# Start of the gated delta rule put in another order: key roots and decay rows beside the last input products, keys normalised before the masks, pooled rows split at other places

## The chip, the cores and the metric

One core of one Trainium2 chip runs the whole program. The metric is the device time of one execution in microseconds (us). PE is TensorE, ACT is ScalarE, DVE is VectorE, POOL is GpSimd, SP is SyncE. PSUM is the accumulator memory of eight banks, each 128 partitions by 512 fp32 values.

## The reference, cut to what matters

Two transformer blocks run over 256 tokens of width 2048. The first begins with a mixer: one product `p = h @ w_in` (5136 columns) gives the pooled part `u`, the gate logits and q, k, v, z of a gated delta net with 8 heads of 128. The delta net, in chunks of 64 tokens:

```python
qkv = silu(causal_dwconv(concat([q, k, v]), conv_w))
q = l2_normalize(q) * Dh ** -0.5
k = l2_normalize(k)
beta = sigmoid(b_logit)
g = -exp(a_log) * softplus(a_logit + dt_bias)
gc = cumsum(g within a chunk)
decay = exp(where(causal, gc[i] - gc[j], -inf))
l_mat = where(strict, beta[i] * (k k^T) * decay, 0)
sol = triangular_solve(l_mat, [v * beta, k * beta * exp(gc)])   # unit diagonal
attn = (q k^T) * decay
q_dec = q * exp(gc); k_dec = k * exp(gc[-1] - gc); chunk_decay = exp(gc[-1])
# then a scan over the 4 chunks, a norm, a gate by silu(z)
```

The mixer's output is `concat([y_pool, y_dn]) @ w_mix_out`. Cross attention, a feed-forward part and a second block with its own attention and feed-forward part follow; nothing in them is touched by the change.

## The kernel before, in words

**Large products.** A fp32 product is made of three fp32r products. `product` (lines 866 to 868) multiplies the split activation (`hhi`, `hlo`) by a weight split into `whi` and `wlo`. SP loads weights in units of four 128-row tiles into four `raw` slots; ACT casts half a unit to `whi` (`split_hi`, line 1322), DVE subtracts to get `wlo` (`split_lo`, line 1813), and PE multiplies. The four `whi` and four `wlo` buffers are the eight 1024-column pieces of `ring`. Results go to the four banks of `GP`: even blocks to banks 0 and 1, odd blocks to banks 2 and 3, and ACT copies them to `p1` (`store`, line 1399), which counts `evac0` for even and `evac1` for odd blocks.

**Input product.** The phases wi0 to wi4 are w_in, wi4 the last. Beside them run the pooling, the gate inputs and six groups of the convolution. For group g: PE turns q/k/v columns into bank pair `TA` (`conv_turn`), ACT makes the first tap (`tap`), DVE adds three taps (`conv`, semaphore `cv_c`), ACT takes the sigmoid into `csg` (`conv_sigmoid`, line 1448, `cv_s`), POOL multiplies (line 756, `cv_m`), PE turns back into `TB` (`conv_back`, `cv_b`), ACT stores into `p1` (`conv_store`, line 1453, `cv_e`). The order is written by hand: `todo` tables on PE, ACT and DVE say behind which unit of which phase each step stands. The number is a unit count; 28 to 31 are units of wi4, and 32 stands behind the cast of its last unit. Two steps of group 5 (sigmoid and store on ACT, `conv_back(5)` on PE) stand behind wi4.

**Delta rule, beginning.** Tokens are two halves (`hf`) of 128, each holding two chunks; all eight heads of a half are handled at once in tiles of 128 by 8 by 128. `AB[hf]` are the two PSUM bank pairs of a half: `TA` and `TB` for half 0, `GP` 0-1 and `GP` 2-3 for half 1. `DN[hf]` names the SBUF tiles (KB, KBT, KT, QT, DT, LT, YY, TT, MT, AA). For half 0 the first eight lie in `ring`, and MT is `flat`. For half 1 they lie in the arena where the pooling and convolution buffers were. The steps in the order before:

1. PE: sums of the log decays, 16 products of 8 columns (`dn_sum`, line 997); then `conv_back(5)`; then differences of log decays, two products of 512 and eight of 128 columns in each half of a bank pair (`dn_diff`, lines 1006 and 1010), which read a row tile that DVE writes (`dn_tg`, line 1967, into KB).
2. ACT: `conv_sigmoid(5)`, `conv_store(5)`, square roots of the key and query norms (`dn_rt`, line 1483), two casts of pooled rows to `hhi` (`pool_hi`, line 1486), exponentials of the sums (`dn_ex`, line 1489), exponentials of the masked differences (`dn_dt`, line 1492).
3. DVE: masks (`dn_dm`, line 1970), then per half: reciprocal, keys normalised (line 1975), keys times beta into KB (`dn_kb`, line 1976), queries normalised (`dn_qn`, line 1978).
4. PE: turns of k and KB (`dn_t`), ACT copies (`dn_tc`, line 1503) to KT and KBT; turns of q, copies to QT; products KT by KBT (`dn_lt_mm`, line 1031) and KT by QT (`dn_at_mm`, line 1036); turns of the decayed q (copies in halves, lines 1500 and 1501).
5. DVE: L (`dn_lt`, line 1982), q times its decay (`dn_qd`, line 1986), the remainder of the pooled rows into `hlo` (`pool_lo`, line 1992), the attention weights (`dn_at`, line 1995).
6. POOL masks L by level (line 761, `lv_m`). PE turns the first level (`lv_z`), DVE subtracts it from the identity (lines 2000 and 2001), and five levels of two products each invert the triangle (lines 1059 and 1072; DVE line 2009).

The solution, the scan over chunks (lines 1084 to 1115) and the product with `w_mix_out` follow. Its first units are the pooled rows and wait for `pool_lo`.

Of the kernel before, what the change touches and what calls it, by code (L numbers as in the profile page):

```python
# [6 lines left out]
F32 = mybir.dt.float32  # L7
F32R = mybir.dt.float32r
ALU = mybir.AluOpType
ACT = mybir.ActivationFunctionType  # L10
# [136 lines left out]
def program(nc, A, out):  # L147
    PH = plan()
    order = list(PH.values())
    with ExitStack() as ctx:  # L150
# [119 lines left out]
        def hd(hf, j):  # L270
# [6 lines left out]
              dict(zip(keys, late[0:7] + [hd(1, 0), late[7], late[2], late[2]]))]  # L277
        ar = Arena(); ar.at = norm_at
# [560 lines left out]
        def _(pe):  # L839
# [122 lines left out]
            def conv_back(g):  # L962
                pe.wait_ge(S("cv_m"), g + 1)
                if g:
                    pe.wait_ge(S("cv_e"), g)
                else:
                    pe.wait_ge(S("pool_f"), 4)
                for h in range(NH):
                    for f in range(4):
                        m = turn(TB[:, h * 512 + f * P:h * 512 + f * P + P], cbuf[g % 3][:, f, h * P:h * P + P])  # L970
                m.then_inc(S("cv_b"), 1)
# [72 lines left out]
            for hf in range(NH):  # L1044
                pe.wait_ge(S("dn_at"), hf + 1)
# [28 lines left out]

            level(0, False, False)
# [235 lines left out]
        def _(act):  # L1311
# [138 lines left out]
            def conv_store(g):  # L1450
                act.wait_ge(S("cv_b"), g + 1)
                c = QKV + 512 * g
                nc.scalar.copy(p1[:, :, c:c + 512], v(TB, 512)).then_inc(S("cv_e"), 1)
# [8 lines left out]
                    30: [lambda it: conv_store(4)]}  # L1462
# [9 lines left out]
            conv_sigmoid(5)  # L1472
# [8 lines left out]
            for hf in range(NH):  # L1481
                act.wait_ge(S("dn_ms"), hf + 1)
                nc.scalar.activation(r16[hf], m16[hf], ACT.Sqrt).then_inc(S("dn_rt"), 1)
            hp = hhi[:, 0:8, :].rearrange("p (a f) t -> p f a t", f=2)
            for f in range(2):
                nc.scalar.copy(hp[:, f, :, :], p1[:, f, 0:1024].rearrange("p (a t) -> p a t", t=T)).then_inc(S("pool_hi"), 1)
            for hf in range(NH):
                act.wait_ge(S("dn_sum"), hf + 1)
                nc.scalar.activation(ex[hf], AB[hf][0][:, 0, 0:32], ACT.Exp).then_inc(S("dn_ex"), 1)
# [3 lines left out]
            for step in ((0, 1), (2,), (3,)):  # L1493
                for hf in range(NH):
                    for j in step:
                        act.wait_ge(S("dn_t"), 2 * hf + j + 1 if j < 2 else hf + 2 * j + 1)
# [16 lines left out]

            level(0, False)
# [269 lines left out]
        def _(dve):  # L1784
# [152 lines left out]
            def squares(hf, i):  # L1937
# [4 lines left out]

            todo = {12: [lambda it: gate_first()], 14: [lambda it: gate_second()], 19: [lambda it: squares(0, 0)],
                    23: [lambda it: squares(1, 0)], 27: [lambda it: squares(0, 1)], 31: [lambda it: squares(1, 1)]}
# [9 lines left out]
            dve.wait_ge(S("gp_b"), 1)  # L1954

# [6 lines left out]
            for hf in range(NH):  # L1962
                nc.vector.tensor_scalar(m16[hf], s16[hf], EPS, None, ALU.add).then_inc(S("dn_ms"), 1)
            for e in range(2):
                dve.wait_ge(S(f"evac{e}"), 1 + PH["wi4"].ev1)
            for hf in range(NH):
                TTo(DN[hf]["KB"], rows(C("upto"), 8), cols(gdec[:, hf * 8:hf * 8 + 8], P), ALU.mult).then_inc(S("dn_tg"), 1)
# [3 lines left out]
            for hf in range(NH):  # L1971
                q3, k3 = hd(hf, 0), hd(hf, 1)
                dve.wait_ge(S("dn_rt"), hf + 1)
                link(nc.vector.reciprocal(i16[hf], r16[hf]))
                link(TTo(k3, k3, cols(i16[hf][:, 8:16], P), ALU.mult))
                TTo(DN[hf]["KB"], k3, cols(beta[:, hf * 8:hf * 8 + 8], P), ALU.mult).then_inc(S("dn_kb"), 1)
                link(nc.vector.tensor_scalar(i16[hf][:, 0:8], i16[hf][:, 0:8], P ** -0.5, None, ALU.mult))
# [9 lines left out]
            for hf in range(NH):  # L1987
                if hf == 0:
                    hp, lp = (t[:, 0:8, :].rearrange("p (a f) t -> p f a t", f=2) for t in (hhi, hlo))
                    for f in range(2):  # L1990
                        dve.wait_ge(S("pool_hi"), f + 1)
                        TTo(lp[:, f, :, :], p1[:, f, 0:1024].rearrange("p (a t) -> p a t", t=T), hp[:, f, :, :].bitcast(F32),
                            ALU.subtract).then_inc(S("pool_lo"), 1)
# [19 lines left out]
            level(4, "AA")  # L2013

# [365 lines left out]
```

## Time and profile before

| | us |
|---|---|
| median of three runs | 2829.23 |
| lowest and highest | 2820.55, 2829.27 |
| the profiled execution's own time | 2826.76 |
| span of its trace | 2825.0 |
| last product of wi4 begins | 259.14 |
| first level of the inversion begins on DVE | 303.70 |
| first product with w_mix_out begins | 381.29 |

All times in rows are us from the start of the span unless they are marked ns. A timeline row has start, duration, engine, line, operation, output<-inputs, shapes and count, and in brackets how long the engine had been idle before it and who ended that. The share of a granted clock of 1.00 is the upper level of TensorE's clock.

### The profile page before, as it was taken

The numbers are of one execution on the slowest core, as the hardware profiler recorded it, in microseconds if no ns is written. First come the engines' busy times: TensorE is split into PE (matmuls) and PEld (weight loads), VectorE is DVE, ScalarE is ACT, GpSimd is POOL, SyncE is SP. The second block draws the span as 40 slices with busy tenths as digits, with TensorE's granted clock in tenths as the row PEclk, the third lists the DMA queues.
The fourth block names the chain that finished last, engine by engine and source line by source line (L and its number), as shares of the span: only waits on it lengthen the run. The fifth ranks groups of instructions, "written<-read, shape, count | busy, mean of one in ns | idle before, by whom it ended". The sixth has DMA issues, their size and how long they took to land.

```text
span 2825.0 us, 34772 instructions
## 1 busy us (share of the span) xinstructions
PE 2742.2 (97%) x13302; PEld 2342.0 (83%) x13302; DVE 1776.7 (63%) x2014; ACT 1326.9 (47%) x1678; POOL 169.6 (6%) x132
## 2 busy tenths in 40 slices
PE   8998899999899999999999999998989999999998
PEld 8998888888788888888888889887778888888886
DVE  4466578676558887865555564546775756644555
ACT  5554354454335545434554544436454444344453
POOL 0001620000000000000000000820000000000000
PEclk9999999999999999999999999999999999999999
DMA  8553048887557787776555556650655866755553
GB/s 282 161 174 122 1 182 286 292 269 267 193 173 269 273 283 265 285 253 194 193 189 197 186 184 201 200 169 5 226 192 182 282 220 226 266 189 180 188 188 119
DMA packets 293266, 579.60 MB, mean 205 GB/s; under 512 B 9168, under 2 KB 46192, under 8 KB 292112
## 3 DMA queue, kind: packets, MB, share of 16 engines
q1 hardware_dynamic: 291296, 566.08, 59.9%
q0 software_dynamic: 1120, 8.57, 0.7%
q10 hardware_dynamic: 720, 3.15, 0.3%
q8 instruction: 90, 1.47, 0.2%
q14 instruction: 40, 0.33, 0.0%
HBM read 575.66 MB, written 2.10 MB: 205 GB/s over the span
## 4 chain that ended last, share of the span: by engine, by line
PE 95%; DVE 3%; ACT 1%; issue 1%; DMA 0%; POOL 0%; SPq 0%; DVEq 0%; ACTq 0%
PE GP L866 28%; PE GP L868 28%; PE GP L867 28%; PE TA L841 2%; PE TB L841 2%; PE TB L489 1%; PE GP L466 1%; PE TA L1229 0%; PE GP L841 0%; DVE x L2248 0%; PE TA L1072 0%; PE GP L1072 0%; PE GP L1059 0%; DMA x<-in_x 0%; PE TA L1279 0%
## 5 line engine op out<-in xcount | busy, mean ns | idle before, releaser
L1813 DVE TENSOR_TENSOR wlo<-raw,whi 128x1024 fp32r<-128x1024 f32 (+2 forms) x904 | 1088.2, 1217 | 811.1 <-ACT whi L1322 801.9
L1322 ACT CAST whi<-raw 128x1024 fp32r<-128x1024 f32 (+2 forms) x904 | 925.8, 1031 | 1167.9 <-PE GP L868 1113.9
L866 PE MATMUL GP<-whi,hhi 128*128 128x512 f32 (+2 forms) x1792 | 688.8, 384 | 3.4 <-issue 2.9
L868 PE MATMUL GP<-whi,hlo 128*128 128x512 f32 (+2 forms) x1792 | 680.3, 380 | 0.0
L867 PE MATMUL GP<-wlo,hhi 128*128 128x512 f32 (+2 forms) x1792 | 679.9, 379 | 0.0
L866 PEld LDWEIGHTS GP<-whi,hhi 128*128 128x128 f32 x1792 | 337.8, 188 | 54.2 <-issue 4.9
L868 PEld LDWEIGHTS GP<-whi,hlo 128*128 128x128 f32 x1792 | 337.3, 188 | 52.0
L867 PEld LDWEIGHTS GP<-wlo,hhi 128*128 128x128 f32 x1792 | 337.8, 189 | 50.3 <-issue 1.0
L866 PE MATMUL GP<-whi,bhi 128*128 128x512 f32 x704 | 276.7, 393 | 0.2 <-DVE blo L1874 0.2
L1801 DVE SCALAR_TENSOR_TENSOR ada_acc<-raw,csig,ada_acc 128x512 f32<-128x512 f32 x360 | 270.3, 751 | 10.2
L868 PE MATMUL GP<-whi,blo 128*128 128x512 f32 x704 | 274.3, 390 | 0.0
L867 PE MATMUL GP<-wlo,bhi 128*128 128x512 f32 x704 | 273.9, 389 | 0.0
L866 PE MATMUL GP<-whi,f2hi 128*128 128x512 f32 x512 | 201.4, 393 | 0.0
L868 PE MATMUL GP<-whi,f2lo 128*128 128x512 f32 x512 | 199.4, 389 | 0.0
L867 PE MATMUL GP<-wlo,f2hi 128*128 128x512 f32 x512 | 199.2, 389 | 0.0
L868 PEld LDWEIGHTS GP<-whi,blo 128*128 128x128 f32 x704 | 132.1, 188 | 27.8
L866 PEld LDWEIGHTS GP<-whi,bhi 128*128 128x128 f32 x704 | 132.2, 188 | 27.2 <-DVE blo L1874 0.7
L867 PEld LDWEIGHTS GP<-wlo,bhi 128*128 128x128 f32 x704 | 132.3, 188 | 26.5
L866 PE MATMUL GP<-whi,fhi 128*128 128x512 f32 x352 | 137.3, 390 | 0.0
L868 PE MATMUL GP<-whi,flo 128*128 128x512 f32 x352 | 137.0, 389 | 0.0
L867 PE MATMUL GP<-wlo,fhi 128*128 128x512 f32 x352 | 136.9, 389 | 0.0
L866 PEld LDWEIGHTS GP<-whi,f2hi 128*128 128x128 f32 x512 | 96.1, 188 | 20.6 <-issue 1.0
(420 smaller groups left out, 2590.8 us busy)
## 6 DMA issues: line engine op xcount, KB each, us to landing
raw<-in_w_up SPq DMA_DIRECT2D x108, 1024.0 KB, 5.4
raw<-in_w_down SPq DMA_DIRECT2D x108, 1024.0 KB, 5.1
raw<-in_w_ada SPq DMA_DIRECT2D x96, 1024.0 KB, 5.3
raw<-in_w_gate SPq DMA_DIRECT2D x44, 1024.0 KB, 5.3
raw<-in_w_in SPq DMA_DIRECT2D x48, 856.0 KB, 4.8
raw<-in_w_xkv SPq DMA_DIRECT2D x32, 1024.0 KB, 5.7
raw<-in_w_in SPq DMA_DIRECT2D x24, 1024.0 KB, 5.1
raw<-in_w_in SPq DMA_DIRECT2D x24, 864.0 KB, 4.7
```

Of the source, the lines that this page charges most:

```text
L466: m = pe.matmul(o[:, h * T:h * T + u["L"]], l, r, start=(d == 0), stop=(d == n - 1), skip_group_check=True)
L489: m = pe.matmul(bank[:, j * P:j * P + P], l, r, start=(d == 0), stop=(d == len(terms) - 1), skip_group_check=True)
L841: return pe.transpose(dst, src, ident[0:n, 0:n] if n != P else ident)
L866: pe.matmul(o, ahi[:, kt, t], whi[r][:, k, 0:q.width], start=first, stop=False)
L867: pe.matmul(o, ahi[:, kt, t], wlo[r][:, k, 0:q.width], start=False, stop=False)
L868: m = pe.matmul(o, alo[:, kt, t], whi[r][:, k, 0:q.width], start=False, stop=last)
L1322: nc.scalar.copy(whi[(2 * g + s) % NRING][:, :, 0:q.width], raw[j % NSLOT][:, 2 * s:2 * s + 2, 0:q.width])\
L1801: m = nc.vector.scalar_tensor_tensor(ada_acc[:, :], raw[j % NSLOT][:, k, :], c, ada_acc[:, :], ALU.mult, ALU.add)
L1813: TTo(wlo[r][:, :, 0:q.width], raw[j % NSLOT][:, 2 * s:2 * s + 2, 0:q.width], whi[r][:, :, 0:q.width].bitcast(F32), ALU.subtract).then_inc ...
```

## The change

On PE, `conv_back(5)` goes ahead of the sums and writes `TA` instead of `TB`. The sums of both halves go to `GP` bank 0 and wait for `evac0` alone. The differences read `TG`, a new name for two tiles (MT of half 0, KBT of half 1). The turns of k of both halves come ahead of those of KB, the turns of q of both ahead of the first products. The wait for `dn_at` is ahead of the first level, no longer ahead of the turns of MT.

On ACT, `conv_sigmoid(5)` stands behind unit 31, the square roots (`key_roots`) at 32, ahead of the last `store`. The two casts of pooled rows stand just ahead of the levels. The copies go by step and half rather than by half and step for the first two.

On DVE, `square_means` follows the last squares, the decay rows are written before the delta rule's other steps, without a wait for `evac`. Keys are normalised and multiplied by beta ahead of the masks, queries behind them. The pooled remainders stand behind the last level.

```diff
+        TG = [DN[0]["MT"], DN[1]["KBT"]]
@@ PE
+                back = TB if g < 5 else TA
+                if g == 5:
+                    pe.wait_ge(S("cv_c"), 6)
...
-            for e in range(2):
-                pe.wait_ge(S(f"evac{e}"), 1 + PH["wi4"].ev1)
-            pe.wait_ge(S("cv_c"), 6)
+            conv_back(5)
+            pe.wait_ge(S("evac0"), 1 + PH["wi4"].ev1)
             for hf in range(NH):
                 for j, m_ in enumerate(("upto", "after", "chunk0", "chunk1")):
-                    m = pe.matmul(AB[hf][0][:, 0, 8 * j:8 * j + 8], C(m_), gdec[:, hf * 8:hf * 8 + 8], start=True, stop=True)
+                    m = pe.matmul(GP[:, 0, 32 * hf + 8 * j:32 * hf + 8 * j + 8], C(m_), gdec[:, hf * 8:hf * 8 + 8], start=True, stop=True)
                 m.then_inc(S("dn_sum"), 1)
-            conv_back(5)
             for hf in range(NH):
-                KB, B8 = DN[hf]["KB"], AB[hf][1]
+                KB, B8 = TG[hf], AB[hf][1]
                 if hf == 0:
-                    pe.wait_ge(S("cv_e"), 6)
+                    pe.wait_ge(S("cv_e"), 5)
+                else:
+                    pe.wait_ge(S("evac1"), 1 + PH["wi4"].ev1)
...
             for hf in range(NH):
-                pe.wait_ge(S("dn_ex"), hf + 1)
+                pe.wait_ge(*((S("dn_ex"), 2) if hf else (S("cv_e"), 6)))
                 pe.wait_ge(S("dn_kb"), hf + 1)
                 for h in range(8):
                     m = turn(AB[hf][0][:, h, :], hd(hf, 1)[:, h, :])
                 m.then_inc(S("dn_t"), 1)
+            for hf in range(NH):
                 pe.wait_ge(S("dn_dm"), hf + 1)
...
-                pe.wait_ge(S("dn_tc"), 2 * hf + 1)
+                pe.wait_ge(S("dn_tc"), hf + 1)
                 pe.wait_ge(S("dn_qn"), hf + 1)
...
-                pe.wait_ge(S("dn_tc"), 2 * hf + 2)
+            for hf in range(NH):
+                pe.wait_ge(S("dn_tc"), hf + 3)
...
             for hf in range(NH):
-                pe.wait_ge(S("dn_at"), hf + 1)
                 pe.wait_ge(S("dn_tc"), hf + 7)
...
+            pe.wait_ge(S("dn_at"), 2)
             level(0, False, False)
@@ ACT
+            def key_roots():
+                for hf in range(NH):
+                    act.wait_ge(S("dn_ms"), hf + 1)
+                    nc.scalar.activation(r16[hf], m16[hf], ACT.Sqrt).then_inc(S("dn_rt"), 1)
...
-                    30: [lambda it: conv_store(4)]}
+                    30: [lambda it: conv_store(4)], 31: [lambda it: conv_sigmoid(5)], 32: [lambda it: key_roots()]}
...
-            conv_sigmoid(5)
             conv_store(5)
...
             for hf in range(NH):
-                act.wait_ge(S("dn_sum"), hf + 1)
-                nc.scalar.activation(ex[hf], AB[hf][0][:, 0, 0:32], ACT.Exp).then_inc(S("dn_ex"), 1)
+                act.wait_ge(S("dn_sum"), 2)
+                nc.scalar.activation(ex[hf], GP[:, 0, 32 * hf:32 * hf + 32], ACT.Exp).then_inc(S("dn_ex"), 1)
...
-            for step in ((0, 1), (2,), (3,)):
+            for step in ((0,), (1,), (2,), (3,)):
...
+            hp = hhi[:, 0:8, :].rearrange("p (a f) t -> p f a t", f=2)
+            for f in range(2):
+                nc.scalar.copy(hp[:, f, :, :], ...).then_inc(S("pool_hi"), 1)      # removed ahead of dn_ex
             level(0, False)
@@ DVE
-                    ..., 31: [lambda it: squares(1, 1)]}
+                    ..., 31: [lambda it: (squares(1, 1), square_means())]}
...
             dve.wait_ge(S("gp_b"), 1)
+            decay_rows()              # TG[hf] = upto * gdec, dn_tg
...
             for hf in range(NH):
+                k3 = hd(hf, 1)
+                dve.wait_ge(S("dn_rt"), hf + 1)
+                link(nc.vector.reciprocal(i16[hf], r16[hf]))
+                link(TTo(k3, k3, cols(i16[hf][:, 8:16], P), ALU.mult))
+                if hf == 0:
+                    for e in range(2):
+                        dve.wait_ge(S(f"evac{e}"), 1 + PH["wi4"].ev1)
+                TTo(DN[hf]["KB"], k3, cols(beta[:, hf * 8:hf * 8 + 8], P), ALU.mult).then_inc(S("dn_kb"), 1)
+                link(nc.vector.tensor_scalar(i16[hf][:, 0:8], i16[hf][:, 0:8], P ** -0.5, None, ALU.mult))
             for hf in range(NH):
                 dve.wait_ge(S("dn_diff"), hf + 1)
                 TTo(DN[hf]["DT"], AB[hf][1], rows(C("chunk_mask"), 8), ALU.add).then_inc(S("dn_dm"), 1)
             for hf in range(NH):
-                ...                   # the key steps above stood here
+                q3 = hd(hf, 0)
                 TTo(q3, q3, cols(i16[hf][:, 0:8], P), ALU.mult).then_inc(S("dn_qn"), 1)
...
             level(4, "AA")
+            for f in range(2):        # removed ahead of dn_at
+                dve.wait_ge(S("pool_hi"), f + 1)
+                TTo(lp[:, f, :, :], ..., hp[:, f, :, :].bitcast(F32), ALU.subtract).then_inc(S("pool_lo"), 1)
+            dve.wait_ge(S("pool_lo"), 2)
```

## Rows read from the trace of the kernel before

**Rows 1.** The page's chain that ended last, share of the span by engine.

```profile
PE 95%; DVE 3%; ACT 1%; issue 1%; DMA 0%; POOL 0%; SPq 0%; DVEq 0%; ACTq 0%
```

**Rows 2.** Windows: length, busy us of PE, PEld, DVE, ACT, POOL, PEclk, DMA share, GB/s.

```profile
260.00:264.00 4.00, 1.92 (x16) 1.86 (x16) 3.23 (x2) 1.61 (x3) 2.31 (x1) 1.00 0.00 0
264.00:268.00 4.00, 2.65 (x9) 1.82 (x10) 1.27 (x1) 1.98 (x2) 0.19 (x1) 0.57 0.01 4
276.00:280.00 4.00, 0.43 (x4) 0.24 (x3) 3.46 (x4) 1.06 (x1) 0.00 (x0) 1.00 0.00 0
280.00:284.00 4.00, 2.61 (x16) 2.24 (x16) 3.90 (x6) 1.85 (x2) 0.00 (x0) 0.70 0.00 0
310.00:352.00 42.00, 41.08 (x366) 40.89 (x367) 13.54 (x20) 18.43 (x35) 32.25 (x24) 1.00 0.00 1
400.00:440.00 40.00, 40.00 (x188) 33.24 (x187) 33.83 (x41) 20.50 (x25) 0.44 (x1) 1.00 0.97 352
```

**Rows 3.** Timeline of PE, from the last product of wi4 to the differences.

```profile
259.14 0.36 PE L868 MATMUL GP<-whi,hlo 128*128 128x428 f32 x1
260.92 1.03 PE L997 MATMUL TA<-small,cst 128*128 128x8 f32 x8 [1.42 <-ACT p L1399]
264.25 1.72 PE L841 MATMUL TB<-cst,cbuf 128*128 128x128 f32 x8 [1.40 <-POOL cbuf L756]
267.06 2.08 PE L1006 MATMUL TB<-ring,cst 128*128 128x512 f32 x2 [1.10 <-ACT p L1453]
...
272.76 1.02 PE L1006 MATMUL GP<-t,cst 128*128 128x512 f32 x2
...
275.38 1.05 PE L1010 MATMUL GP<-cst,t 128*128 128x128 f32 x8
```

**Rows 4.** Timeline of PE, from the key products to the first level.

```profile
289.09 1.95 PE L1031 MATMUL TB<-ring 128*128 128x128 f32 x16
...
297.11 1.04 PE L841 MATMUL TB<-cst,p 128*128 128x128 f32 x8
...
302.55 1.97 PE L841 MATMUL TB<-cst,flat 128*128 128x128 f32 x8 [3.53 <-DVE ring L1995]
...
306.39 1.16 PE L1059 MATMUL TA<-ring,flat 128*128 128x128 f32 x8 [0.45 <-POOL flat L761]
```

**Rows 5.** Timeline of ACT, 250 to 299 us.

```profile
250.25 0.91 ACT L1322 CAST whi<-raw 128x856 fp32r<-128x856 f32 x1 [1.36 <-PE GP L868]
259.54 1.13 ACT L1399 ACTIVATE p<-GP,small 128x428 f32<-128x428 f32 x2 [8.37 <-PE GP L868]
260.55 1.06 ACT L1448 ACTIVATE csg<-cbuf 128x1024 f32<-128x1024 f32 x1
...
267.03 1.28 ACT L1483 ACT_TABLE_LOAD   x1
...
277.73 1.06 ACT L1492 ACTIVATE t<-t 128x1024 f32<-128x1024 f32 x1 [2.45 <-DVE t L1970]
281.62 1.01 ACT L1503 COPY ring<-TA 128x1024 f32<-128x1024 f32 x1 [2.83 <-PE TA L841]
...
298.18 0.59 ACT L1500 COPY ring<-TB 128x512 f32<-128x512 f32 x1 [5.22 <-PE TB L841]
```

**Rows 6.** Timeline of POOL, 261 to 296 us.

```profile
261.69 2.50 POOL L756 TENSOR_TENSOR cbuf<-cbuf,csg 128x1024 f32<-128x1024 f32 x1 [21.99 <-ACT csg L1448]
292.45 3.41 POOL L761 TENSOR_TENSOR flat<-ring,cst 128x512 f32<-128x512 f32 x2 [28.26 <-DVE ring L1982]
```

**Rows 7.** Timeline of DVE, 252 to 361 us.

```profile
252.16 1.22 DVE L1940 TENSOR_TENSOR flat<-p 128x1024 f32<-128x1024 f32 x1
...
261.91 3.36 DVE L1967 TENSOR_TENSOR t<-cst,small 128x1024 f32<-128x1024 f32 x1
...
276.47 1.23 DVE L1970 TENSOR_TENSOR t<-GP,cst 128x1024 f32<-128x1024 f32 x1 [2.28 <-PE GP L1010]
...
291.15 1.23 DVE L1982 TENSOR_TENSOR ring<-TB,ring 128x1024 f32<-128x1024 f32 x1 [5.41 <-PE TB L1031]
...
296.87 4.49 DVE L1992 TENSOR_TENSOR hlo<-p,hhi 128x1024 fp32r<-128x1024 f32 x2
...
303.70 0.69 DVE L2000 TENSOR_TENSOR ring<-cst,TB 128x512 f32<-128x512 f32 x1
...
360.66 0.69 DVE L2034 COPY p<-TB 128x512 f32<-128x512 f32 x1 [7.54 <-PE TB L1112]
```

More of the change, by code:

```diff
@@ L967, in conv_back @@
                     pe.wait_ge(S("pool_f"), 4)
+                back = TB if g < 5 else TA
+                if g == 5:
+                    pe.wait_ge(S("cv_c"), 6)
                 for h in range(NH):
                     for f in range(4):
-                        m = turn(TB[:, h * 512 + f * P:h * 512 + f * P + P], cbuf[g % 3][:, f, h * P:h * P + P])
+                        m = turn(back[:, h * 512 + f * P:h * 512 + f * P + P], cbuf[g % 3][:, f, h * P:h * P + P])
                 m.then_inc(S("cv_b"), 1)
@@ L1452, in conv_store @@
                 c = QKV + 512 * g
-                nc.scalar.copy(p1[:, :, c:c + 512], v(TB, 512)).then_inc(S("cv_e"), 1)
+                nc.scalar.copy(p1[:, :, c:c + 512], v(TB if g < 5 else TA, 512)).then_inc(S("cv_e"), 1)
+            def key_roots():
+                for hf in range(NH):
+                    act.wait_ge(S("dn_ms"), hf + 1)
+                    nc.scalar.activation(r16[hf], m16[hf], ACT.Sqrt).then_inc(S("dn_rt"), 1)
             todo = {2: [lambda it: pool_mean(0)], 3: [lambda it: tap(0)], 4: [lambda it: (pool_out(0), pool_mean(1))],
@@ L1481, in _ @@
             for hf in range(NH):
[L1482 to L1487, printed above, removed]
-                act.wait_ge(S("dn_sum"), hf + 1)
-                nc.scalar.activation(ex[hf], AB[hf][0][:, 0, 0:32], ACT.Exp).then_inc(S("dn_ex"), 1)
+                act.wait_ge(S("dn_sum"), 2)
+                nc.scalar.activation(ex[hf], GP[:, 0, 32 * hf:32 * hf + 32], ACT.Exp).then_inc(S("dn_ex"), 1)
             for hf in range(NH):
@@ L1492, in _ @@
                 nc.scalar.activation(DN[hf]["DT"], DN[hf]["DT"], ACT.Exp).then_inc(S("dn_dt"), 1)
-            for step in ((0, 1), (2,), (3,)):
+            for step in ((0,), (1,), (2,), (3,)):
                 for hf in range(NH):
                     for j in step:
-                        act.wait_ge(S("dn_t"), 2 * hf + j + 1 if j < 2 else hf + 2 * j + 1)
+                        act.wait_ge(S("dn_t"), hf + 2 * j + 1)
                         if j == 3:
@@ L1512, in level @@
                             nc.scalar.copy(DN[hf]["AA"][:, a, :], AB[hf][1][:, a, :]).then_inc(S("lv_ac"), 1)
+            hp = hhi[:, 0:8, :].rearrange("p (a f) t -> p f a t", f=2)
+            for f in range(2):
+                nc.scalar.copy(hp[:, f, :, :], p1[:, f, 0:1024].rearrange("p (a t) -> p a t", t=T)).then_inc(S("pool_hi"), 1)
             level(0, False)
@@ L1941, in squares, with square_means, decay_rows @@
                 link(nc.vector.tensor_reduce(s16[hf][:, 8 * i:8 * i + 8], sq, AX.X, ALU.add))
+            def square_means():
+                for hf in range(NH):
+                    nc.vector.tensor_scalar(m16[hf], s16[hf], EPS, None, ALU.add).then_inc(S("dn_ms"), 1)
+            def decay_rows():
+                for hf in range(NH):
+                    TTo(TG[hf], rows(C("upto"), 8), cols(gdec[:, hf * 8:hf * 8 + 8], P), ALU.mult).then_inc(S("dn_tg"), 1)
             todo = {12: [lambda it: gate_first()], 14: [lambda it: gate_second()], 19: [lambda it: squares(0, 0)],
-                    23: [lambda it: squares(1, 0)], 27: [lambda it: squares(0, 1)], 31: [lambda it: squares(1, 1)]}
+                    23: [lambda it: squares(1, 0)], 27: [lambda it: squares(0, 1)], 31: [lambda it: (squares(1, 1), square_means())]}
             for g, at in enumerate((4, 8, 16, 20, 24, 28)):
@@ L1962, in _ @@
             for hf in range(NH):
[L1963 to L1967, printed above, removed]
+                k3 = hd(hf, 1)
[7 more added lines that the diff above has]
+                link(nc.vector.tensor_scalar(i16[hf][:, 0:8], i16[hf][:, 0:8], P ** -0.5, None, ALU.mult))
             for hf in range(NH):
@@ L1971, in _ @@
             for hf in range(NH):
[L1972 to L1977, printed above, removed]
+                q3 = hd(hf, 0)
                 TTo(q3, q3, cols(i16[hf][:, 0:8], P), ALU.mult).then_inc(S("dn_qn"), 1)
@@ L1987, in _ @@
             for hf in range(NH):
[L1988 to L1993, printed above, removed]
                 dve.wait_ge(S("dn_at_mm"), hf + 1)
@@ L2013, in _ @@
             level(4, "AA")
+            hp, lp = (t[:, 0:8, :].rearrange("p (a f) t -> p f a t", f=2) for t in (hhi, hlo))
+            for f in range(2):
+                dve.wait_ge(S("pool_hi"), f + 1)
+                TTo(lp[:, f, :, :], p1[:, f, 0:1024].rearrange("p (a t) -> p a t", t=T), hp[:, f, :, :].bitcast(F32),
+                    ALU.subtract).then_inc(S("pool_lo"), 1)
+            dve.wait_ge(S("pool_lo"), 2)
             def new_values(n):
```

## The prediction, made before the changed kernel was run

> **What bounds the kernel now.** I read the chain that ended last first: 95% of it is TensorE, so time is to be had only where TensorE stands still or runs slowly [rows 1]. The windows then show where that is. In the 40 us after the product with w_mix_out has begun, PE is busy 40.00 of 40.00, and in the levels of the inversion 41.08 of 42.00, both at the upper clock of 2.4 GHz; between them and the end of w_in it is not: 1.92 of 4.00 in 260 to 264, 0.43 of 4.00 in 276 to 280. Behind each of these two idle windows the granted clock is down, 0.57 and 0.70 as means of a stretch that is partly at 1.2 GHz [rows 2]. Third, the timelines of the engines between 259 and 304 say who holds PE: ACT's store, POOL's product of group 5, ACT's store of that group [rows 3], then DVE, which makes masks and keys one behind the other, and at the end again DVE, where the turn of MT waits 3.53 us for the attention weights [rows 4] behind the pooled remainders (two in 4.49 us) [rows 7]. From 303.70, where DVE begins the first level, DVE, POOL and PE run a fixed pattern that the change leaves alone. So the sum is one date: when does DVE begin that level?
>
> The remaining wi4 products end at 259.50 in either kernel (last row 259.14, 0.36 long, the next instruction can begin at about 259.35) [rows 3].
>
> **Part 1, up to the differences.** Removed from the path: 1.42 us for the store, 1.40 us for POOL, 1.10 us for ACT's store of group 5 [rows 3]. For that the sigmoid must be early. The last cast ends at 251.16 and ACT is then idle for 8.37 us until 259.54 [rows 5]: the sigmoid runs 251.1 to 252.2 (1.06), POOL multiplies until 254.7 (2.50) [rows 6]. Cover is 4.6 us against the turn at 259.35; without it the turn would wait as before. The roots stand ahead of the last store in ACT's queue, so a late root would hold `evac1`. DVE's squares begin at 252.16 (product 1.22, reduction about as long), the means are there at 255.0, table load (1.28) already past, roots done at 255.3. Should POOL's product hold DVE's first square, it costs at most the 2.14 us that the decay row lost in the same company (3.36 instead of 1.22) [rows 7]: roots at 257.5, still 2 us early. Nothing is queued behind but the store itself. The decay rows (2 times 1.14 behind each other) are there at 257.4, at worst 259.6; PE asks at 262. The first key product is then done at 259.9 at the latest or waits one pitch more; KB of half 0 starts when the store ends, 260.77, KB of half 1 is there at 265 (or 266).
>
> PE's new path: eight turns from 259.35, 0.87 us at the upper clock as the turns of q show by start to start (1.04 long, with 0.17 overlap) [rows 4]: 260.2. Sixteen sums: eight took 0.88 start to start, so 1.76 [rows 3]: 262.0. Their bank 0 was emptied long before. Differences: half 1 took 272.76 to 276.43, 3.67 us, at the upper clock; half 0 took 267.06 to 272.76, 5.70 us, partly at the lower [rows 3]. I take 3.6 for each, since PE now has no gap from 259 on: 269.2, against 276.43 before. This step is 7.2 us earlier, of it 3.9 from idle time, 0.9 from the turns (1.72 to 0.87), 2.1 from the differences, and the rest handovers. Bounds: if both differences run as the first did before, 273.4; the least is 3.5 each, 269.0.
>
> The clock is the one unmeasured thing here. In the rows the lower level follows windows in which PE was busy for a half or less [rows 2]. The Trainium skill, TensorE: Matmul & The Clock Gate, Part 1, says that the clock is held at its lower level by default and released by activity, according to how busy TensorE was; the trace agrees so far. By that rule the removal of the gaps brings the 2.4 GHz that I take. The same section calls the moment of the switch variable from run to run. If that moment, and not the gaps, rules here, the cost stays, and that is the first rival.
>
> **Part 2, masks and keys.** Before, mask 1, reciprocal, key product, KB and query of half 0 and then of half 1 lay between the differences and the key products: 276.43 to 289.09, 12.7 us. Now only the mask, an exponential and ACT's copies do. From the end e = 269.2: DVE masks half 1 at e + 0.0, ACT's exponential begins e + 1.3 (276.47 to 277.73 in the rows [rows 5, 7]) and frees ACT at e + 2.3; KT0, KT1 and KBT0 are copied, 0.95 apart and the last 1.01 long [rows 5]: e + 5.2. PE meanwhile turns k (2 times 0.87), KB (2 times 0.87), q of half 0 behind KT0's copy, q of half 1 behind KT1's at e + 4.2 to e + 5.1. ACT and PE arrive together, so the product KT by KBT of half 0 begins at e + 5.3 = 274.5, 14.6 us earlier than 289.09 [rows 4]. ACT's store of group 5, the exponential's table (1.28) and `dn_ex` are done at 263.4, under the differences (PE asks at 270.1); without that cover 1.3 us more. DVE's two query products (1.14 each) end at e + 3.5, before their turns. What is late next is ACT: a bound above is PE waiting for all four copies, 0.95 more; below, PE's turns alone, e + 4.5.
>
> **Part 3, up to the first level.** Products of L, half 0 and half 1, and of attention, half 0 and half 1: each 16 matmuls in 1.79 us start to start (1.95 long) [rows 4]. 274.5 + 4 times 1.79 + 0.15 = 281.8. Decayed q turned: ACT begins its two half copies 1.07 us after the turn began (297.11, 298.18) and needs 0.48 + 0.59 [rows 4, 5]: 284.0. PE turns the first half of MT, 0.45, and with the handover DVE can begin at 284.65. DVE's own line: L0 at 276.6 (2.06 behind PE's start, 289.09 to 291.15 [rows 4, 7]), decayed q0 277.7, L1 278.85, decayed q1 280.0 to 281.2, or until 282.4 if POOL's two maskings (3.41 with DVE in the way, 1.2 each alone [rows 6]) hold it; attention weights of half 0 and half 1 behind PE at 281.9, or until 284.7. Both lines end at about 284.7. Before it was 303.70 [rows 7]: **19.0 us earlier**. Left out of this line are the pooled remainders: 4.49 us on DVE [rows 7]. They go behind the last level, where DVE is idle 7.54 us before the scan [rows 7]; they need about 2.3 us there, because POOL is idle too. If that cover were gone, up to 4.5 us return. The casts go to ACT between 285 and 287; its first copy of a level comes 1.2 us behind PE's first product, which moves from 306.39 to 287.4 [rows 4]: cover about 1.6 us, and if it is missed, 1 us at most. The removed wait for `dn_at` costs nothing where it now stands: DVE has passed it by then.
>
> **Sum.** Everything behind depends on what runs before it and on no fixed date, transfers included: the four slots of w_mix_out were filled by 258, and the later ones are issued as slots come free. The profiled execution took 2826.76 us; 2826.76 - 19.0 = 2807.8. The median of the three runs is 2829.23, 2.5 above that execution, and gives 2810.2. I predict 2809. The steps' bounds add up to a gain of 14.8 (differences at the lower clock) to 20 us (PE's turns alone).
>
> **Rivals.**
> First, *the clock still falls*. The sums have eight columns and PE does little in them. If they count as idleness, the differences run at 1.2 GHz: half 0 needs 5.7 instead of 3.6, half 1 the same: 4.2 us lost, 2813. For: the fall before came behind exactly these sums. Against: behind 1.42, 1.40 and 1.10 us of idleness too, which go.
> Second, *the gain doesn't arrive*. A transfer or another engine has its own date: the stretch behind carries 352 GB/s at a DMA share of 0.97 [rows 2]. If it were bound by transfers, starting 19 us earlier would show as waits of PE: 2829, or 2821 to 2835 as the three runs scatter. Against: PE busy 40.00 of 40.00 there, and no transfer of it beyond the four slots can start before the delta rule is over, so the ratio of the two doesn't change.
> Third, *slower*. The levels run close to saturation at 1.00 [rows 2]. If the new order started them at 1.2 GHz and the pattern's short gaps kept the clock there, each us of the levels' PE work costs one more. It decides from 19 us of such work on; over all of the 41.08 us the balance is +22, 2849 for 2827. For: the first products of the levels come singly with gaps of 0.7 us. Against: the same gaps stood there before, behind the same turns, and the clock was 1.00.
>
> **How the numbers follow.** Forecast as summed 0.78; clock still falls 0.11 (also faster); gain doesn't arrive 0.07; slower 0.04. A measurement of this kernel can tell about 0.3%, 8.5 us, from no change. Faster by more: 0.90 (0.78 + 0.11, and what of the second lands beyond the bound); within: 0.06; slower: 0.04. The range goes from 2800 (the lowest run, 2820.55, less 20) to 2818 (the highest, 2829.3, less 15, and some of what the second rival might take).
>
> **What would show it.** One row each in the profile of the changed kernel: turns from `cbuf` right behind the last wi4 product and lasting 0.9; granted clock 1.00 from 256 to 276; L1006's successor beginning at 262; the key products at 274 to 275; the first level on DVE at 284 to 286; PE's first w_mix_out product at 362 instead of 381.29; DVE's remainders in the gap before the scan. It is wrong if the sigmoid of group 5 or the roots end behind 259, if the clock is at 0.5 in the differences, or if the first w_mix_out product is early and the end is not.

## The result and the profile after

| | before | after |
|---|---|---|
| median of five runs, us | 2828.34 | 2801.84 |
| lowest and highest | 2817.66, 2829.27 | 2800.70, 2810.06 |
| profiled execution's own time | 2826.76 | 2801.02 |
| span of its trace | 2825.0 | 2799.2 |
| from the last wi4 product to the first level on DVE | 44.56 | 25.30 |
| from the last wi4 product to the first w_mix_out product | 122.15 | 102.88 |
| from there to the end of the span | 2443.7 | 2436.7 |

The two medians are 26.5 us apart. The ratio on record, 0.9931, with a 95% interval from 0.9906 to 0.9956, is 19.5 us, between 12 and 27; the reason why the two differ stands below, with the last seven microseconds. The interval leaves out 1, so the changed kernel is faster, by less than 1%. The chain is still 95% PE. PE's timeline now runs without a hole from wi4 to the turn of MT.

```profile
260.06 1.13 ACT L1405 ACTIVATE p<-GP,small 128x428 f32<-128x428 f32 x2 [3.50 <-PE GP L869]
...
283.15 0.59 ACT L1504 COPY ring<-TB 128x512 f32<-128x512 f32 x1 [5.63 <-PE TB L842]
```

These are two rows of ACT's timeline of the changed kernel; PE's, with the last wi4 product first, is:

```profile
259.67 0.36 PE L869 MATMUL GP<-whi,hlo 128*128 128x428 f32 x1
259.86 1.03 PE L842 MATMUL TA<-cst,cbuf 128*128 128x128 f32 x8
260.73 1.85 PE L1000 MATMUL GP<-small,cst 128*128 128x8 f32 x16
262.44 1.10 PE L1010 MATMUL TB<-flat,cst 128*128 128x512 f32 x2
...
266.02 1.02 PE L1010 MATMUL GP<-t,cst 128*128 128x512 f32 x2
...
269.53 1.04 PE L842 MATMUL TA<-cst,p 128*128 128x128 f32 x8
...
274.85 2.03 PE L1037 MATMUL TB<-ring 128*128 128x128 f32 x16
...
284.28 1.09 PE L842 MATMUL TB<-cst,flat 128*128 128x128 f32 x8 [0.29 <-ACT ring L1505]
...
287.71 1.13 PE L1064 MATMUL TA<-ring,flat 128*128 128x128 f32 x8 [1.36 <-issue]
```

Against [rows 3, 4] the three idle stretches of 1.42, 1.40 and 1.10 us ahead of the differences are gone, and L1037, which stood at 289.09 as L1031, stands at 274.85. The turn from `cbuf` begins 0.19 us behind the start of the last product and lasts 1.03 us (0.87 to the next start), where it lasted 1.72 us before [rows 3].

The windows of the changed kernel (length, busy of PE, PEld, DVE, ACT, POOL, PEclk, DMA share, GB/s):

```profile
256.00:260.00 4.00, 4.00 (x23) 3.84 (x22) 3.93 (x7) 0.32 (x2) 0.17 (x1) 1.00 0.36 137
260.00:264.00 4.00, 4.00 (x33) 3.52 (x32) 2.78 (x5) 3.60 (x6) 0.00 (x0) 1.00 0.00 0
264.00:268.00 4.00, 4.00 (x25) 3.01 (x25) 2.71 (x4) 0.45 (x1) 0.00 (x0) 1.00 0.00 0
284.00:288.00 4.00, 2.36 (x18) 2.04 (x19) 3.03 (x4) 3.09 (x5) 2.49 (x2) 1.00 0.00 0
293.00:333.00 40.00, 39.66 (x356) 39.66 (x357) 12.59 (x19) 18.01 (x34) 31.10 (x23) 1.00 0.00 1
362.00:366.00 4.00, 3.53 (x10) 2.76 (x9) 4.00 (x3) 1.00 (x1) 2.58 (x1) 0.57 0.25 43
380.00:420.00 40.00, 40.00 (x186) 33.18 (x186) 34.02 (x41) 20.52 (x25) 0.77 (x1) 1.00 0.94 346
```

Where [rows 2] had 1.92 busy of 4.00 and then a clock of 0.57, there is now 4.00 of 4.00 and 1.00. The product with w_mix_out is as busy as before (40.00 of 40.00), so the 19 us are not given back there. The window from 362 to 366, with its start, ran at 0.57 in this execution; the first four us of that product ran at 1.00 in the profile of the kernel before (381.29 to 385.29) and in the second one of the changed kernel (362.29 to 366.29).

DVE's timeline of the changed kernel shows what became of its work:

```profile
256.39 1.22 DVE L1956 TENSOR_TENSOR flat<-cst,small 128x1024 f32<-128x1024 f32 x1
...
261.32 1.23 DVE L1986 TENSOR_TENSOR ring<-p,small 128x1024 f32<-128x1024 f32 x1 [1.15 <-ACT p L1405]
...
269.73 1.23 DVE L1990 TENSOR_TENSOR t<-GP,cst 128x1024 f32<-128x1024 f32 x1 [2.21 <-PE GP L1014]
...
280.39 1.22 DVE L2001 TENSOR_TENSOR p<-p,small 128x1024 f32<-128x1024 f32 x1
...
284.97 0.69 DVE L2009 TENSOR_TENSOR ring<-cst,TB 128x512 f32<-128x512 f32 x1 [1.10 <-PE TB L842]
...
334.29 2.35 DVE L2026 TENSOR_TENSOR hlo<-p,hhi 128x1024 fp32r<-128x1024 f32 x2
341.99 1.52 DVE L2049 COPY p<-TB 128x512 f32<-128x512 f32 x2 [5.34 <-PE TB L1118]
```

The first level (L2009) waits 1.10 us for PE instead of following the attention weights; before, DVE was the last to come [rows 7]. The two remainders take 2.35 us where they took 4.49 [rows 7], and DVE still idles 5.34 us behind them.

### The profile page after: what moved, and what is told of

Same layout as the page of the kernel before. It is cut to its first block, busy times and chain, and to the rows that moved or that the text cites. A ratio compares the mean times of both kernels' runs of the same rounds, so it can differ in the third digit from the quotient of the medians.

```text
span 2799.2 us, 34774 instructions
## 1 busy us (share of the span) xinstructions
PE 2727.0 (97%) x13302; PEld 2328.3 (83%) x13302; DVE 1772.5 (63%) x2014; ACT 1324.0 (47%) x1678; POOL 169.6 (6%) x132
## 4 chain that ended last, share of the span: by engine, by line
PE 95%; DVE 3%; ACT 1%; issue 1%; DMA 0%; SPq 0%; POOL 0%; DVEq 0%; ACTq 0%
PE GP L867 29%; PE GP L869 28%; PE GP L868 28%; PE TA L842 2%; PE TB L842 2%; PE TB L490 1%; PE GP L467 1%; PE TA L1235 0%; DVE x L2263 0%; DVE wlo L1820 0%; PE GP L1077 0%; PE TA L1077 0%; PE GP L1064 0%; PE GP L842 0%; DMA x<-in_x 0%
## 5 line engine op out<-in xcount | busy, mean ns | idle before, releaser
L868 PEld LDWEIGHTS GP<-wlo,f2hi 128*128 128x128 f32 x512 | 96.1, 188 | 20.6 <-issue 1.0
```

Source lines behind the costliest of these rows:

```text
L868: pe.matmul(o, ahi[:, kt, t], wlo[r][:, k, 0:q.width], start=False, stop=False)
```

## The experiments

Each experiment below was profiled once. Most are read by one distance, from the start of the last wi4 product to the first level on DVE (44.56 us before, 25.30 after, 25.30 again in a second profile of the changed kernel; 44.56 and 43.99 for the two profiles of the kernel before). It contains nothing but the part that was changed, and it repeats to 0.6 us or better, where a single whole time can be 10 us off. Read up to the first w_mix_out product instead, each distance gives nearly the same comparison, at most 1.1 us away: gap_one, for one, has 6.03 us there instead of 4.99, chiefly because 16 matmuls of its scan took 3.63 us where the changed kernel took 2.05.

| kernel | distance | beside its neighbour | first w_mix_out product to the end |
|---|---|---|---|
| before, twice | 44.56, 43.99 | | 2443.7, 2444.8 |
| after, twice | 25.30, 25.30 | | 2436.7, 2445.0 |
| gaps_back | 31.66 | after + 6.36 | 2445.9 |
| gap_one | 30.29 | after + 4.99 | 2445.9 |
| sigmoid_late | 35.54 | after + 10.24 | 2435.2 |
| roots_late | 26.14 | after + 0.84 | 2436.1 |
| keys_late | 33.74 | after + 8.44 | 2444.6 |
| pooled_old | 28.56 | after + 3.26 | 2435.9 |
| sigmoid_alone | 41.49 | before - 3.07 | 2445.9 |
| keys_alone | 35.73 | before - 8.83 | 2445.9 |
| pooled_alone | 40.80 | before - 3.76 | 2436.1 |
| identity_ahead | see below | | 2443.6 |

### Does the clock fall because of the gaps?

**gaps_back** puts waits of PE back into the changed kernel:

```diff
+            for e in range(2):
+                pe.wait_ge(S(f"evac{e}"), 1 + PH["wi4"].ev1)
             conv_back(5)
-            pe.wait_ge(S("evac0"), 1 + PH["wi4"].ev1)
+            pe.wait_ge(S("cv_e"), 6)
```

> The changed kernel, but PE waits for the last store of wi4 before it turns group 5 back, and for the store of group 5 before the sums: two short gaps as before, about 1.4 and 1.0 us, nothing else moved. Distance from the last wi4 product to the first level on DVE: 25.30 us in the changed kernel. Theory (idle gaps make the clock fall): granted clock at 1.2 GHz somewhere in the differences, distance 25.3 + 2.4 + 2 to 4 = 30 to 32 us. Rival (the moment rules, not the gaps): clock stays at 2.4 GHz, distance 27.7. Stretch from the first w_mix_out product to the end of the span: 2436.7 us in the changed kernel, 2443.7 in the one before; if the difference of 7.0 comes from the change it is 2436 to 2437 here, if it is scatter of the clock it is anything from 2432 to 2447.

31.66 us: the two gaps, 1.48 and 1.10 us of idleness, put off what stands behind them by 1.65 and 1.30 us, and the lower clock makes up the remaining 3.4 of the 6.36. **gap_one** keeps only the first:

```diff
+            for e in range(2):
+                pe.wait_ge(S(f"evac{e}"), 1 + PH["wi4"].ev1)
             conv_back(5)
-            pe.wait_ge(S("evac0"), 1 + PH["wi4"].ev1)
```

> The changed kernel, but PE waits for the last store of wi4 before it turns group 5 back: one gap of about 1.4 us, the second gap of gaps_back (1.10 us) is not there. Question: how little idleness brings the fall. If one such gap is enough, the granted clock falls in the differences as in gaps_back (31.66 us) and the distance is 29 to 31 us; if it takes both, the clock stays at 2.4 GHz and the distance is 26.7.

One gap is enough. PE's timeline and the windows of gap_one:

```profile
261.47 1.06 PE L842 MATMUL TA<-cst,cbuf 128*128 128x128 f32 x8 [1.48 <-issue]
262.37 2.73 PE L1001 MATMUL GP<-small,cst 128*128 128x8 f32 x16
264.95 2.06 PE L1011 MATMUL TB<-flat,cst 128*128 128x512 f32 x2
```

```profile
256.00:260.00 4.00, 3.99 (x21) 3.53 (x19) 3.93 (x7) 0.32 (x2) 0.13 (x1) 1.00 0.34 132
260.00:264.00 4.00, 2.53 (x20) 2.56 (x20) 2.78 (x5) 2.54 (x4) 0.00 (x0) 0.89 0.02 4
264.00:268.00 4.00, 4.00 (x14) 2.97 (x14) 1.44 (x3) 1.17 (x3) 0.00 (x0) 0.50 0.00 0
268.00:272.00 4.00, 4.00 (x18) 2.61 (x17) 0.75 (x1) 0.00 (x0) 0.00 (x0) 0.76 0.00 0
```

The sums take 2.73 instead of 1.85 us and the first two products of the differences 2.06 instead of 1.10; of the 4.99 us 1.65 are the gap (the turn begins 1.84 us behind the last product instead of 0.19) and 3.3 the lower clock. Beside gap_one, the second gap of gaps_back costs 1.37 us, which is about its own length. The rival by which the moment alone rules falls: in the six profiles with PE unbroken here (after twice, roots_late, pooled_old, keys_late, identity_ahead) the granted clock was 1.00 from 256 to 268, and in the eight with a gap there it fell each time, before 268. No run has this short gap without the narrow sums behind it, so what share these have is not shown. And a gap alone doesn't decide either. Behind the turn of MT the changed kernel has gaps of 1.36, 0.72, 0.74 and 0.73 us. In its first profile the clock stayed at 1.00 there; in the second it fell at 289 and cost nothing, since PE waits for POOL there anyway (distance from the last wi4 product to the second product of level 0: 34.67 and 34.70).

### The sigmoid and the roots beside the last products

**sigmoid_late** takes both steps out of the tables:

```diff
-    30: [lambda it: conv_store(4)], 31: [lambda it: conv_sigmoid(5)], 32: [lambda it: key_roots()]}
+    30: [lambda it: conv_store(4)]}
...
+            conv_sigmoid(5)
             conv_store(5)
+            key_roots()
```

> The changed kernel, but the sigmoid of group 5 and the square roots of the norms stand behind the last store of wi4 again. Theory: PE's turn of group 5 waits until about 5 us behind the last wi4 product (store 1.0, sigmoid 1.06, POOL 2.5), keys wait for the roots (about 9 us behind it), the clock falls: distance to the first level 31.5 to 34 us instead of 25.3. Rival (the beginning is covered by the later chain of ACT copies and DVE): under 28 us. Stretch behind the first w_mix_out product: as said for the first run, 2436 to 2437 or scattered.

35.54 us, above the range of the theory. PE stands 4.74 us, until POOL's product is there (262.90, 2.34 long), and then does the turn, the sums and the first half of the differences at the lower clock; from the turn to the end of the differences 15.0 us pass instead of 9.7. The later start, 4.9 us, and the slower course, 5.3, are the whole 10.24:

```profile
265.45 1.94 PE L842 MATMUL TA<-cst,cbuf 128*128 128x128 f32 x8 [4.74 <-issue]
267.18 3.42 PE L1000 MATMUL GP<-small,cst 128*128 128x8 f32 x16
```

**roots_late** puts only `key_roots()` back behind `conv_store(5)` (the hook 32 goes, the sigmoid's stays).

> The changed kernel, but the square roots stand behind the store of group 5; the sigmoid stays early. It parts the 10.2 us that sigmoid_late cost (35.54 against 25.30). Theory: roots at 264 instead of 256, KB of half 1 at 269 instead of 265.4, masks behind it; PE has work until 269.5, so distance 26 to 27.5 us, and most of the 10.2 belongs to the sigmoid. Rival (the roots were the greater part): 30 us or more.

26.14 us, 0.84 more. The early roots are worth under 1 us, because PE has work of its own until 269.5. What the late roots put off is DVE's first mask (269.78 instead of 266.30), with it ACT's exponentials and copies, and PE waits once, for the first copy:

```profile
274.18 1.09 PE L842 MATMUL TA<-cst,p 128*128 128x128 f32 x8 [0.64 <-ACT ring L1508]
```

With the roots late, the late sigmoid costs another 9.4 us (35.54 against 26.14).

**sigmoid_alone** is the same move in the kernel before: `31: [lambda it: conv_sigmoid(5)]` added, the call behind wi4 removed.

> The kernel before with one part of the change: the sigmoid of group 5 stands behind unit 31 instead of behind the last store. PE's order is the old one, so the turn of group 5 now follows the sums at once, about 3.6 us behind the last wi4 product instead of 5.1. Theory (the parts help mostly together): differences begin 2.4 us earlier, distance to the first level 40 to 42.5 us instead of 44.56. Rival (POOL's product was the wait of the whole beginning): under 39 us.

41.49 us, 3.07 less. The same step that costs 9.4 us when it is undone in the changed kernel is worth 3.07 in the kernel before. There the gaps of 1.42 and 1.10 us remain, and the lower clock with them: the granted clock of sigmoid_alone was 0.62 and 0.52 in 264 to 268 and 268 to 272.

### Keys ahead of the masks

**keys_late** exchanges two blocks on DVE in the changed kernel: the masks (`dn_dm`) first, then the key steps.

> The changed kernel, but DVE normalises the keys and makes KB behind the masks. Theory: PE waits for KB of half 0 about 4 us, LT begins 5 us later, and the idle stretch brings 1.2 GHz for a part: distance 30.5 to 33 us instead of 25.3. Rival (ACT's exponentials and copies bound that stretch anyway): under 27.5 us.

33.74 us. The theory holds; the distance lies 0.7 us above its range. PE stands 4.09 us for the first KB, and then, which I had not priced, 1.70 us for the second; the rest, about 2.5 us, is the lower clock on the turns behind, as two of its windows show.

```profile
272.00:276.00 4.00, 1.19 (x8) 0.85 (x8) 3.90 (x5) 1.04 (x2) 0.00 (x0) 0.92 0.00 0
276.00:280.00 4.00, 2.56 (x12) 2.59 (x13) 3.71 (x5) 1.37 (x2) 0.00 (x0) 0.50 0.00 0
```

```profile
277.44 1.94 PE L842 MATMUL GP<-cst,p 128*128 128x128 f32 x8 [1.70 <-DVE t L1989]
```

**keys_alone** does it in the kernel before:

```diff
+        TG = [DN[0]["MT"], DN[1]["KBT"]]
-                KB, B8 = DN[hf]["KB"], AB[hf][1]
+                KB, B8 = TG[hf], AB[hf][1]
-                TTo(DN[hf]["KB"], rows(C("upto"), 8), ...).then_inc(S("dn_tg"), 1)
+                TTo(TG[hf], rows(C("upto"), 8), ...).then_inc(S("dn_tg"), 1)
+            (reciprocal, key product, KB and scaling of both halves)
             (masks of both halves)
+            (queries of both halves)
```

> The kernel before with one part of the change: DVE normalises the keys and makes KB ahead of the masks (decay rows in the tiles of TG, at their old time; roots, pooled rows, sigmoid and PE's order as before). Theory: half of the work between the differences and LT goes under the differences; DVE waits for the roots until 268.6, masks end at about 276.5, LT begins about 5 us earlier: distance 38 to 41 us instead of 44.56. Rival (without early roots the keys only trade places with the masks): 43 us or more.

35.73 us, better than expected: 8.83 us of the 19.26. I had let the masks hold PE, but when the differences end both KB are there (DVE is done with the second at 276.21), and PE turns keys at once (277.65, right behind the last difference of 276.76). In the kernel before, PE stood twice at that place:

```profile
280.52 1.06 PE L841 MATMUL TA<-cst,p 128*128 128x128 f32 x8 [4.09 <-DVE ring L1976]
284.54 1.94 PE L841 MATMUL GP<-cst,p 128*128 128x128 f32 x8 [1.41 <-DVE t L1976]
```

So 5.5 of the 8.83 us are idle time, and most of the other 3.3 are the lower clock of the turns (0.50 in 284 to 288 before; 1.00 from 276 to 292 in keys_alone). This part needs neither early roots nor a new order of PE.

### The pooled rows

**pooled_old** puts casts and remainders back to their old places in the changed kernel, **pooled_alone** moves them in the kernel before; both edits are the pooled lines of the change, one backwards.

> The changed kernel, but the casts of the pooled rows stand ahead of the exponentials of the sums on ACT, and the pooled remainders ahead of the attention weights on DVE, as before. Theory: DVE begins the attention weights 2.3 to 4.5 us later (POOL masks beside it), the first level begins 3.3 us later: distance 28 to 29.5 us. Rival (the remainders fit into DVE's gaps and the level is set by PE and ACT): under 26.5 us.

> The kernel before with one part of the change: casts of the pooled rows ahead of the levels on ACT, remainders behind the last level on DVE. Undoing it in the changed kernel cost 3.26 us (28.56 against 25.30). Theory (the part is additive): distance 40 to 41.5 us instead of 44.56. Rival (it is worth more beside the others): 43 us or more.

28.56 us (3.26 more than after) and 40.80 (3.76 less than before): additive within 0.5 us, as expected. In pooled_old DVE needs 4.51 us for the pair:

```profile
282.18 4.51 DVE L2005 TENSOR_TENSOR hlo<-p,hhi 128x1024 fp32r<-128x1024 f32 x2
286.61 1.21 DVE L2009 TENSOR_TENSOR ring<-TA,ring 128x1024 f32<-128x1024 f32 x1
```

and 2.35 in the place where POOL rests (it stands idle for 18.66 us up to 342.76). POOL's two masks beside the 4.51 us took 4.47 us; in the changed kernel they took 2.52, beside DVE products of which one input comes from PSUM (L2004, 1.21 and 1.22). The Trainium skill, SBUF — State Buffer, section "Who interferes with whom", says that a DVE instruction with two inputs in SBUF contends with a GpSimd instruction that reads SBUF, and calls their shared port pair an exclusive lock; the durations agree with that.

### Where the other seven microseconds come from

> The changed kernel once more, as it is. Distance from the last wi4 product to the first level on DVE 25.3 us, as in its first profile (fixed by the program). Stretch from the first w_mix_out product to the end: 2436.7 in its first profile. Theory (the 7.0 us beyond the predicted 19 are scatter of TensorE's clock in later stages): anything from 2432 to 2447, with the time at the lower clock to match, and a ratio of 0.991 to 0.996. Rival (they come from the change): 2436 to 2437 again, ratio 0.990 to 0.991.

> The kernel before once more, as it is. Distance 44.6 us. Stretch behind the first w_mix_out product 2443.7 in its first profile. Scatter theory: anything from 2432 to 2447. Rival: 2443 to 2444 again.

The changed kernel again: 2801.53 us median of six (2801.15 to 2810.89), ratio 0.9928, interval 0.9904 to 0.9951, so by its expectation the ratio is inside the scatter theory's band. Its profile gives 2445.0 us behind the first w_mix_out product, not 2436.7: one program, two values 8.3 us apart, so the rival of after_again falls. The kernel before again gives 2444.8, near its first 2443.7, and tells nothing by itself. Over all 14 profiles the stretch is 2435.2 to 2436.7 in five and 2443.6 to 2445.9 in nine, and it does not go with the date at which it begins: pooled_alone begins it at 379.32 with 2436.1, the second profile of the changed kernel at 362.29 with 2445.0. Windows of the changed kernel's first and second profile, over the two attention stages and the one behind:

```profile
725.00:800.00 75.00, 64.95 (x358) 56.83 (x357) 34.03 (x42) 26.93 (x44) 0.00 (x0) 0.95 0.35 121
1895.00:1995.00 100.00, 86.59 (x513) 73.02 (x514) 71.86 (x139) 56.27 (x165) 0.00 (x0) 0.98 0.24 80
2050.00:2100.00 50.00, 37.78 (x178) 31.63 (x177) 37.07 (x60) 29.42 (x48) 0.00 (x0) 0.90 0.40 136
```

```profile
725.00:800.00 75.00, 64.96 (x337) 56.52 (x337) 31.79 (x39) 24.31 (x42) 0.00 (x0) 0.89 0.30 101
1895.00:1995.00 100.00, 87.88 (x498) 76.64 (x497) 66.77 (x138) 52.96 (x158) 0.00 (x0) 0.90 0.18 64
2050.00:2100.00 50.00, 38.35 (x178) 32.19 (x178) 40.20 (x66) 28.23 (x49) 0.00 (x0) 0.86 0.45 149
```

Over the same microseconds of nearly the same work the mean clock is 0.95 or 0.89, 0.98 or 0.90, 0.90 or 0.86. The whole executions have 0.993 and 0.988; as an estimate, 0.005 of 2800 us is 14 us of work at the upper clock, which is room enough for the 8.3, since a part of the lower clock falls on waits. The mean granted clock of a whole run sorts the times of one kernel too. In the later series of 11 runs the kernel before ran five times with 0.983 (2829.3 to 2830.2 us, mean 2829.9) and five times with 0.989 or 0.990 (2816.1 to 2820.6, mean 2818.1), and once with 0.986 (2827.6); the changed kernel, in its 11 of both series, seven times with 0.991 to 0.993 (2800.7 to 2801.8, mean 2801.3) and four times with 0.988 to 0.990 (2807.8 to 2810.9, mean 2809.5). Upper group against upper group the change gives 20.4 us, lower against lower 16.8, in the middle the 19 of the distance. The first medians, 2828.34 and 2801.84, happen to be an upper and a lower value; 7.0 of the 25.8 us between the two first traces lie in code that is the same in both.

### One step further

**identity_ahead** uses DVE's idle 1.10 us before the first level:

```diff
                 for e in range(2):
                     a = slice(4 * e, 4 * e + 4)
+                    dve.wait_ge(S("lv_m"), 2 * hf + e + 1)
+                    TTo(DN[hf]["AA"][:, a, :], rows(ident, 4), DN[hf]["MT"][:, a, :], ALU.subtract).then_inc(S("lv_ac"), 1)
+                for e in range(2):
+                    a = slice(4 * e, 4 * e + 4)
                     dve.wait_ge(S("lv_z"), 2 * hf + e + 1)
                     TTo(DN[hf]["TT"][:, a, :], ...).then_inc(S("lv_u"), 1)
-                    TTo(DN[hf]["AA"][:, a, :], ...).then_inc(S("lv_ac"), 1)
@@ POOL, level 1
+                        if lv == 1:
+                            g.wait_ge(S("lv_z"), 2 * hf + e + 1)
```

> The changed kernel with one step further: DVE takes MT from the identity (AA) for both quarters of a half ahead of the subtractions from PSUM (TT), so that it uses its idle 1.1 us before the first level; POOL's first masks of level 1 wait for the turn of MT as well. The fourth group of level 0 products begins 33.67 us behind the last wi4 product in the changed kernel. Theory: 32.3 here, the whole 1.4 us faster than the changed kernel, which the time can't show. Rival (POOL and DVE block each other at other places): 33.7 or more.

The start of the fourth group can't be read, since the records of groups three and four run together. The step behind them, the second product of level 0, begins 33.49 us behind the last wi4 product instead of 34.67 (294.34 in the changed kernel), 1.2 us earlier, near the 1.4 expected. The stage up to w_mix_out is 102.38 us against 102.88, only 0.5 less: in this execution the clock fell in the last step of the scan, where 16 matmuls took 3.27 us instead of 2.05. Whole times, 2806.5 us median (2798.71 to 2809.22), ratio to before 0.9930 (0.9907 to 0.9954), can't tell it from the changed kernel when taken together, as expected. Sorted by mean clock they hint at a gain: the two with 0.992 took 2798.71 and 2799.99 us, below all 11 of the changed kernel, and the four with 0.988 or 0.989 took 2807.7 in the mean against 2809.5. Six runs are too few to call that shown.

## Why the prediction was right

**The sum held.** 19.0 us was forecast, 19.26 came (18.69 if the second profile of the kernel before is taken). Step by step, behind the start of the last wi4 product, forecast and measured: turn of group 5 0.21 and 0.19; sums 1.06 and 1.06; differences 2.9 and 2.77; their end (key turns) 10.1 and 9.86; L products 15.4 and 15.18; turn of MT 24.9 and 24.61; first level 25.6 and 25.30. The part that rested on an assumption, that the differences would need 3.6 us each at the upper clock, measured 3.58 and 3.51. ACT and PE arrived together at the products of L, as worked out (KBT's copy ends at 274.78, PE begins at 274.85 without a wait).

**The covers held.** Sigmoid 251.59 to 252.65, roots ready at 256.6 (forecast 255.3, in a trace whose last product stands 0.53 us earlier), against the last store at 260.06. In the contest between POOL and DVE's squares I had priced only DVE's loss, up to 2.14 us. Both lost: POOL's product took 3.44 us instead of 2.50, and the small DVE step behind the squares 1.08 instead of 0.25, until POOL was done.

```profile
252.73 3.44 POOL L757 TENSOR_TENSOR cbuf<-cbuf,csg 128x1024 f32<-128x1024 f32 x1 [12.51 <-ACT csg L1454]
255.20 1.08 DVE L1952 TENSOR_SCALAR small<-small 128x16 f32<-128x16 f32 x2
```

Neither reached PE, since POOL ended at 256.17, 3.7 us ahead of the turn. The remainders took 2.35 us in DVE's gap, 2.3 were forecast. ACT's casts ended at 287.1, its first copy of a level began at 288.88: cover 1.8 us, forecast 1.6.

**What was off.** The decayed query of half 1 was never held by POOL: 280.39, 1.22 long. POOL's first two masks gave way instead and took 4.46 us. So DVE's line ended at 283.9, 1.1 us before it was needed, and not together with ACT's. And the predicted time, 2809, stands 7 us above the median of 2801.84. The step of it is the turn from the distance to a median: I took the three runs' median as base and treated what lies behind the first w_mix_out product as constant. It is constant in work but not in time; it varies by up to 10.7 us over the 14 profiles, with the granted clock. The gain between the medians, 26.5 us against the 20 of the forecast, is for that reason the sum of a step that was right and of a draw of the clock. The range from 2800 to 2818 had been drawn from the scatter of the runs before and holds the median, but by 1.8 us only; that it does is in part luck.

**The rivals.** *The clock still falls* is refuted for this order and confirmed as a mechanism: with one gap of 1.48 us the sums and the differences do fall to 1.2 GHz, which costs 3.3 us, and 3.4 with the second gap (4.2 was the price given). The sums of eight columns alone don't do it: without the gap the clock stayed at 1.00. *The gain doesn't arrive* is refuted, since PE is busy 40.00 of 40.00 in w_mix_out 19 us earlier. *Slower* needed the levels at 1.2 GHz: they ran at 1.00 in the first profile, and in the second the clock fell only at their start (0.72 and 0.86 in 288 to 292 and 292 to 296) and was back at 1.00 from 296.

**What each part is worth** depends on the others: keys ahead 8.83 us alone and 8.44 at the margin, pooled rows 3.76 and 3.26, sigmoid 3.07 and 9.4. The three alone add up to 15.7 of the 19.3, and to 13.7 when read at the first w_mix_out product. The rest is the new order of PE, the early roots, and what the parts give each other by ending the gaps and the lower clock ahead of the differences; these I have not parted.

What stays open: why the clock of the attention stages takes one course in some executions and another in others, and whether the change shifts the share. Of the 16 runs of the kernel before in both series 9 lie above 2825, of the 11 of the changed kernel 4 above 2805; that tells nothing either way.

## What to carry to other kernels

Where one engine bounds a kernel, the way to price a reordering of its idle stretch is to find one date behind it that nothing else sets, and to follow every engine to that date; here all seven dates came within 0.3 us. A short gap costs more than its length when the instructions behind it run at the lower clock, so of two small waits in a row the last one removed pays most (1.37 us for the first removed, 4.99 for the last), and a part tried by itself can be undersold (the sigmoid, 3.07 against 9.4 us), though the keys and the pooled rows were not. Compare traces by the stretch that was changed, and don't book the difference of two whole times as the effect before another profile of the same kernel has shown how far the rest moves.

## What the runs showed of the hardware

After a single idle stretch of 1.48 us on PE, and behind it a turn and sixteen products of eight columns, the clock was at 1.2 GHz: 0.50 in the window from 264 to 268 of gap_one. Behind gaps of 1.36 and three times 0.7 us a little later in the changed kernel it stayed at 2.4 GHz in the first profile and fell in the second. The Trainium skill, TensorE: Matmul & The Clock Gate, Part 1, says that the clock follows recent activity and that the moment of the switch varies between runs of one program; both agree with these rows, and with the second profile of the changed kernel. That this scatter moves a kernel of 2.8 ms, 97% busy on PE, by 10 to 14 us from run to run was not expected.
